# Forgetting and memory attention computed by key instead of by query, with one output product for all mixer blocks

## What is computed

```
x = x + 1/2 * swiglu_1(rms(x))
h = rms(x);  u, c_gate, b_gate, q, k, v, f_logit, q_mem = split(h @ w_in)
y_conv = b_gate * (conv_b + causal conv over 3 tokens of (c_gate * u))        # 256 columns
q, k = head_rms(q), head_rms(k)                                              # 8 heads x 64
F = cumsum(log_sigmoid(f_logit + b_f))                                       # one value per token and head
y_fox = softmax(q k^T / 8 + F_t - F_s, masked to s <= t) v                    # 512 columns
y_mem = softmax(head_rms(q_mem) mem_k^T / 8) mem_v                            # 4 heads, 256 memory tokens
x = x + concat(y_conv, y_fox, y_mem) @ w_out
x = x + 1/2 * swiglu_2(rms(x));  x = rms(x)
```

## Time and profile before

| | |
|---|---|
| time, median of 3 runs | 2314.63 us (2314.17 to 2317.61) |
| the profiled execution, its own time | 2306.02 us |
| its span | 2304.2 us |
| PE busy | 92% of the span |
| DVE, ACT, POOL busy | 51%, 33%, 17% |
| mean granted clock of PE | 0.96 of full speed |
| mixer (817 to 1499 us of the span) | 682 us |

### The profile page before, as it was taken

The page is one execution under the profiler, slowest core; times in us unless marked ns, Lnnn a source line. Parts: engine busy times, 40 slices in busy tenths (PEclk is TensorE's granted clock), DMA queues, the critical chain, the costliest instruction groups (busy, mean ns, idle before and its releaser), DMA issues.

```text
span 2304.2 us, 40450 instructions
## 1 busy us (share of the span) xinstructions
PE 2118.3 (92%) x15785; PEld 2027.2 (88%) x15785; DVE 1183.0 (51%) x2332; ACT 749.0 (33%) x1385; POOL 388.5 (17%) x290
## 2 busy tenths in 40 slices
PE   4599999999999879899999989966999999999996
PEld 4599999999999879779788777765999999999996
DVE  6855566556320063545544556677655665643103
ACT  5332222324221241152433433443232232433213
POOL 0000000004444422221221223100000000143440
PEclk7799999999999989899999998987999999999997
DMA  4512222228532114311020210132222222385222
GB/s 150 140 57 83 84 81 88 70 77 301 175 123 92 46 29 37 62 29 56 23 79 23 55 51 18 44 113 83 77 73 84 84 75 90 116 297 168 89 68 85
DMA packets 206427, 205.78 MB, mean 89 GB/s; under 512 B 15864, under 2 KB 150264, under 8 KB 206016
## 3 DMA queue, kind: packets, MB, share of 16 engines
q1 hardware_dynamic: 206272, 203.59, 29.1%
HBM read 161.87 MB, written 41.69 MB: 88 GB/s over the span
## 4 chain that ended last, share of the span: by engine, by line
PE 52%; DVE 5%; issue 2%; ACT 2%; DMA 1%; another core or an unknown queue 0%; POOL 0%; DVEq 0%; ACTq 0%; SPq 0%
PE banks L256 14%; PE banks L257 14%; PE banks L258 14%; PE banks L1994 3%; PE banks L2033 3%; PE banks L2014 2%; PE banks L1761 1%; PE banks L1945 1%; DVE xT L1563 1%; DVE row_bias L1641 1%; DMA x_again<-x_spill 1%; DVE w_raw L1708 0%; DVE hforms_lo L1415 0%; DVE hforms_f L1399 0%; PE banks L2096 0%
## 5 line engine op out<-in xcount | busy, mean ns | idle before, releaser
L256 PE MATMUL banks<-hforms_hi,w_hi 128*128 128x264 f32 x2112 | 604.2, 286 | 65.7 <-DVE hforms_lo L1415 44.6
L257 PE MATMUL banks<-hforms_lo,w_hi 128*128 128x264 f32 x2112 | 606.2, 287 | 0.0
L258 PE MATMUL banks<-hforms_hi,w_lo 128*128 128x264 f32 x2112 | 603.0, 286 | 0.0
L256 PEld LDWEIGHTS banks<-hforms_hi,w_hi 128*128 128x128 f32 x2112 | 402.3, 190 | 68.9 <-issue 35.8
L747 POOL TENSOR_TENSOR w_lo<-w_raw,w_hi 128x1024 fp32r<-128x1024 f32 x88 | 219.6, 2498 | 1311.8 <-ACT w_hi L992 1311.8
L258 PEld LDWEIGHTS banks<-hforms_hi,w_lo 128*128 128x128 f32 x2112 | 402.1, 190 | 0.0
L257 PEld LDWEIGHTS banks<-hforms_lo,w_hi 128*128 128x128 f32 x2112 | 401.1, 190 | 0.0
L256 PE MATMUL banks<-acts_a,w_hi 128*128 128x264 f32 x896 | 255.3, 285 | 1.8 <-DVE acts_a L1433 1.8
L258 PE MATMUL banks<-acts_a,w_lo 128*128 128x264 f32 x896 | 255.2, 285 | 0.0
L257 PE MATMUL banks<-acts_a,w_hi 128*128 128x264 f32 x896 | 255.1, 285 | 0.0
L992 ACT ACTIVATE w_hi<-w_raw 128x1024 fp32r<-128x1024 f32 x88 | 93.3, 1060 | 347.8 <-PE banks L258 305.4
(11 more groups left out here) (260 smaller groups left out, 4135.7 us busy)
## 6 DMA issues: line engine op xcount, KB each, us to landing
w_raw<-in_w_ffn_down SPq DMA_DIRECT2D x88, 512.0 KB, 4.0
w_raw<-in_w_ffn_gate SPq DMA_DIRECT2D x48, 512.0 KB, 5.2
w_raw<-in_w_ffn_up SPq DMA_DIRECT2D x48, 512.0 KB, 5.2
act_rows<-act_f SPq DMA_DIRECT2D x44, 528.0 KB, 2.8
acts_f<-act_rows SPq DMA_DIRECT2D x44, 528.0 KB, 5.0
w_raw<-in_w_in SPq DMA_DIRECT2D x20, 512.0 KB, 6.1
x_spill<-xT SPq DMA_DIRECT2D x4, 2112.0 KB, 9.3
xT<-x_spill SPq DMA_DIRECT2D x2, 4224.0 KB, 16.6
```

Source lines behind the costliest of these rows:

```text
L256: eng.matmul(out, w_hi, x_hi, start=first, stop=False, skip_group_check=added)
L257: eng.matmul(out, w_hi, x_lo, start=False, stop=False, skip_group_check=added)
L258: return eng.matmul(out, w_lo, x_hi, start=False, stop=last, skip_group_check=added)
```

## The change

The change rewrites the mixer from the first conv block to the start of feed-forward 2. The feed-forward code is untouched. In parts:

**Output products to the end.** No mixer block has its own output product. Each result `mix_f32` is stored as rows in memory (`mix_rows`, by `store_mix` on SP). At the end SP loads w_out (eight blocks of 128 rows) and the results back; ACT rounds both (`w_out_hi`, `mix_hi`), POOL subtracts for the low parts of w_out, DVE for those of the results (`mix_lo`). One stretch of PE then does three chunks, in each of them eight column blocks d with the blocks of rows (0 to 3), (4 to 6), (7) summed in eight banks; 576 matmuls as before, but 24 additions to x in place of 192. x goes out to memory at the start of the mixer (`x_spill`) and comes back at the end, since the room is used.

**Stacked operands.** With 64 rows a head, a head's high and low parts fit one above the other in 128 partitions. `k_hi_twice` (KS1) holds k_hi in both halves, `k_lo_and_one` (KS2) k_lo in one half and a row of ones in the other; `q_hi_lo` (Q1) q_hi and q_lo, `q_hi_and_max` (Q2) q_hi and one row with minus the row maximum. KS1 with Q1 gives k_hi*q_hi + k_hi*q_lo in one float32r matmul, KS2 with Q2 gives k_lo*q_hi and subtracts the maximum. ACT makes the rounded copies (L1118, L1126), DVE the second copy of k_hi and the low parts.

**Maxima from a one-pass product.** For each of the 18 units PE makes KS1 times Q1 alone (`scores`, L2055, L2058), one query tile by all its keys; DVE takes the maximum with -F as before, but writes nothing that is used (`scores_minusF`). PE turns the column of maxima to a row (`turn_max`), ACT copies it, negated, into Q2 (`maxima`).

**Scores by key.** The scores are then made again with keys on the partitions: 28 blocks of one key tile by up to 512 queries for a fox pair, 12 for a memory pair (`key_blocks`, `keyed`, two matmuls and the mask). ACT takes the exponential with bias -F of the key (L1163) straight into `probsT`, four buffers. No probability is turned.

**Weighted sum with the row sum in it.** `v_and_ones` (VO) holds v of a head in 64 columns and ones in the other 64. `weigh` multiplies it (stationary) by the probabilities (up to 512 columns, plain float32); one half of the bank is the result by feature, the other half the sum in every row. ACT makes a rough reciprocal by Ln and Exp (`sum_rough`), DVE one correction step and the product in three instructions (`mixed`). No result is turned.

**Moves.** The maxima products of head 1 stand among the key blocks of head 0. The fox loop is unrolled. DVE's forget scan stands among the norms of the first fox pair; the turn of log f and -F by token, which stood before the fox loop, comes after the key tiles of the first fox pair. The second conv block uses banks shifted by one. The memory's products 2 and 3 wait for the memory operand (`mp["dve"]`), where this wait stood after product 2. FFN2's means wait for the 24 additions.

The diff, cut to its core:

```diff
-        qz = sb("qT_by_head", [P, PAIR, T], F32, ms_)
...
+        KS1 = sb("k_hi_twice", [P, PAIR, KEYS], F32R, ax)
+        KS2 = sb("k_lo_and_one", [P, PAIR, KEYS], F32R, ax)
+        VO = sb("v_and_ones", [P, NT + 1, PAIR, P], F32, ax)
...
+        Q1 = sb("q_hi_lo", [P, PAIR, T], F32R, xs)
+        Q2 = sb("q_hi_and_max", [P, PAIR, T], F32R, xs)
...
+        PRT = sb("probsT", [P, 4, 512], F32, xs)
...
+        mix_rows = nc.dram_tensor("mix_rows", (KT, P, T), F32, kind="Internal").ap()
...
+        UNITS = [(PT, 0), (PT, 1)] + [(t, j) for j in range(PAIR) for t in range(PT)]
...
+        def key_blocks(kind):
+            r = []
+            for j in range(PAIR):
+                for e in range(PT if kind == "fox" else 2):
+                    for c in range(2):
+                        lo = max(P * e, 512 * c) if kind == "fox" else 512 * c
+                        if lo < 512 * c + 512:
+                            r.append((j, P * e, P, e, lo, 512 * c + 512 - lo, 4 * j + c, lo - 512 * c, e == 0,
...
+        HOOK = {"fox": [[t] for t in range(PT)] + [[]] * 4, "mem": [[0, 1], [2, 3], [4, 5], [6, 7]]}
+        TURN2 = {"fox": 9, "mem": 3}
...
+            def store_mix(b):
+                sp.dma_start(mix_rows[b], mixf[:, :]).then_inc(MIX["stored"], 16)
...
+                def q_hi(c):
...
+                    for q in (Q1, Q2):
+                        for j in range(PAIR):
+                            act.activation(q[half_rows(j), j, s:s + w], qT[half_rows(j), s:s + w], ACT.Copy)\
+                                .then_inc(A["qhi"], 1)
...
+                def exps(n):
...
+                    act.wait_ge(A["keyed"], b0 + n + 1)
+                    if b0 + n >= 4:
+                        act.wait_ge(A["pv"], b0 + n - 3)
...
+                        act.activation(dst, src, ACT.Exp, bias=Ftok[0:kr, vo, it * PAIR + j:it * PAIR + j + 1])\
+                            .then_inc(A["expd"], 1)
...
+                def sum_rough(x):
...
+                    act.activation(lr[r, 0:w], bank(b, w)[r], ACT.Ln).then_inc(A["rough_sum"], 1)
...
+                    act.activation(lr[r, 0:w], lr[r, 0:w], ACT.Exp, scale=-1.0).then_inc(A["rough_sum"], 1)
...
-                        dve.tensor_tensor_reduce(B["prob"][0:rows, a % 2, 0:W], sc, nF[0:rows, j, k0:k0 + W], 1.0,
-                                                 -3e38, ALU.add, ALU.max, m).then_inc(A["smax"], 1)
...
+                        dve.tensor_tensor_reduce(junk[0:rows, 0:w], PS[0:rows, b:b + w], nF[0:rows, j, k0:k0 + w], 1.0,
+                                                 -3e38, ALU.add, ALU.max, m).then_inc(A["smax"], 1)
...
+                def mixed(x):
...
+                    dve.tensor_tensor(lt[l, 0:w], PS[l, b:b + w], lr[l, 0:w], ALU.mult).then_inc(A["mixed"], 1)
...
+                    dve.scalar_tensor_tensor(lt[r, 0:w], lt[l, 0:w], -2.0, lr[l, 0:w], ALU.add, ALU.mult)\
+                       .then_inc(A["mixed"], 1)
...
+                    dve.scalar_tensor_tensor(mixf[r, s:s + w], PS[r, b:b + w], -1.0, lt[r, 0:w], ALU.mult, ALU.mult)\
+                       .then_inc(A["mixed"], 1)
...
-                        mm = pe.matmul(PS[0:rows, base + c:base + c + n], qz[:, j, s:s + rows],
-                                       B["kT"][:, k0 + c:k0 + c + n], start=True, stop=not diag)
...
+                        mm = pe.matmul(PS[0:rows, base + c:base + c + cw], Q1[:, j, s:s + rows],
+                                       KS1[:, j, k0 + c:k0 + c + cw], start=True, stop=not diag)
...
-                def turn_probs(a):
...
-                def turn_o(t):
...
-                        mm = pe.matmul(bank(6 + j, HD, rows), B["pT"][0:kr, a % 2, c:c + rows], v,
-                                       start=(e == 0), stop=(e == len(kb) - 1))
...
+                def keyed(n):
...
+                    if n >= 2:
+                        pe.wait_ge(A["expd"], b0 + n - 1)
...
+                    pe.matmul(dst, KS1[:, j, kc:kc + kr], Q1[:, j, q0:q0 + w], start=True, stop=False)
+                    mm = pe.matmul(dst, KS2[:, j, kc:kc + kr], Q2[:, j, q0:q0 + w], start=False, stop=not diag)
...
+                def weigh(n):
...
+                    pe.wait_ge(A["expd"], b0 + n + 1)
...
+                    pe.matmul(PS[:, 512 * ob + oc:512 * ob + oc + w], VO[0:kr, vo, j, :], PRT[0:kr, (b0 + n) % 4, 0:w],
+                              start=first, stop=last, skip_group_check=True).then_inc(A["pv"], 1)
...
+                for n in range(NB[kind] + 1):
+                    if n < NB[kind]:
+                        keyed(n)
+                    if n:
+                        weigh(n - 1)
+                    if n < len(HOOK[kind]):
+                        for t in HOOK[kind][n]:
+                            scores(2 + PT + t)
+                    if n == TURN2[kind]:
+                        turn_four(1, 0)
+                        turn_four(1, 1)
...
-                out_product(kind, it, (6, 12, 18), (0,))
-                turn_o(NT - 1)
-                out_product(kind, it, (6, 12, 18), (1, 2))
...
+            for c, (s, w) in enumerate(CHUNKS):
+                for ks in ((0, 1, 2, 3), (4, 5, 6), (7,)):
+                    for d in range(KT):
...
+                        for k in ks:
...
+                            mm = split3(pe, bank(OBANK[d], w), h[:, k % 4, ds], l[:, k % 4, ds], hh[:, k, s:s + w],
+                                        hl[:, k, s:s + w], k == 0, k == KT - 1)
```

1275 lines of the change are left out of this document (673 added, 602 removed).

## The result

The changed kernel takes 2341.98 us (median of 4 runs, 2340.95 to 2343.32), against 2314.4 us of the kernel before in the same runs: ratio 1.0121, 95% interval 1.0103 to 1.0138. It is slower by 28 us where 24 less were forecast. The span of its profiled execution is 2338.9 us, 34.7 more than before.

What follows compares the result with a forecast made beforehand. PE, busy 92% of the span, was taken as the bound. Conv -31.7, fox -71.7, memory and output product +79.2 summed to -24.2 us: 2290 us on the median 2314.6, range 2266 to 2316.

Steps and rivals of the forecast that it cites:

- The two prices: PE matmuls: rounded hi/lo operands pass once at 0.453 ns a column, plain f32 four times at 1.7 ns.
- the work of a pair: PE's work in a fox pair's attention after the change: 34.6 us against some 47 before.
- a rival at 2.6 us a pair: Narrow one-pass products in fox pairs cost the four-pass rate: 2300 us in all, chance 10%.
- below the column rate nothing can lie: Narrow one-pass products, 32 to 160 columns, some 40 a fox pair, were priced by columns as the lower end.
- The first maxima product starts 3.8 us after the projections: Fox pair: PE waits for ScalarE's copies, through some 3.5 us after PE, with 0.5 us of transposes to do.
- The clock: Rival: PE's pauses start each pair's loop at 1.2 GHz, 6 us in six pairs, 36 in all: 2326, chance 10%.
- I take 3.6 us of pauses: Fox loop over 28 key blocks: 28.9 us of PE work plus these pauses, 0 to 10 possible.
- First fox pair: 7 us above the other pairs' 83.8: about 4 for the forget scan in VectorE's queue, some 3 for -F.
- POOL's new memsets and the copy of x to memory lie under the products of these blocks: Conv stage: this added work, like storing each block's result, was taken as hidden under PE's products.
- Memory pairs: Two pairs of 62.0 and 60.6 us, each with 7.4 us of copies after the last projection; loop 14.5 in the first.
- Conv, -31.7: Conv stage to the first fox product: 98.3 us instead of 130, with two output products gone.
- Output products: All 576 products in one piece at the end: 92.0 us, 0.6 for the last addition, 2.2 waiting for FFN2's squares.

Runs made afterwards that it cites:

- e1: Changed kernel with GpSimd's split of the next block's weights made after all 18 maxima of the pair, not right after the last projection: 2340.2 us, ratio 1.0108.
- e6: Changed kernel with ScalarE's four copies of the first chunk of q after a fox pair's seventh projection, not its eighth: 2342.4 us, ratio 1.0137.
- e12: e11 with GpSimd's split of the next weights after the maxima, and 12 and 26 extra matmuls in the pauses behind the projections: 2301.9 us, ratio 0.9943.
- e2: Changed kernel with a filler, extra PE matmuls nobody uses, in the pauses before the maxima products and first key block of every pair but the first: 2335.2 us.
- e9: Changed kernel with key block scores made two blocks ahead of the weighted sum, not one, in head 1 and behind it: 2343.0 us, ratio 1.0134.
- e5: e3 with the first pair's cached keys and values loaded ahead of the two small stores of the conv state: 2337.5 us, ratio 1.0104.
- e3: Changed kernel with ScalarE and VectorE waiting for GpSimd's constants at the parts of k, not at the first fox pair's start: 2345.3 us, ratio 1.0127.
- e4: Changed kernel with two buffers in turn for the rough reciprocal of a sum, not one: 2333.9 us, ratio 1.0081.
- e15: e14 with 4 extra matmuls in a memory pair's pause in place of 12: 2292.1 us, ratio 0.9907.
- e13: Kernel before, with the first split of w_out moved behind the squares and sums of the mixer's first norm: 2303.8 us, ratio 0.9954.
- e14: e12 with the first two q chunks' parts made between a memory pair's projections, and 12 extra matmuls in its pause: 2291.0 us, ratio 0.9909.
- e11: e10 with the extra matmuls of e2, 15 in a fox and 34 in a memory pair's pause, then 4 and 3: 2304.9 us, ratio 0.9965.
- e10: Changed kernel with the edits of e4, e5 (which contains e3), e6 and e9 together, without extra matmuls: 2321.9 us, ratio 1.0036.

## Why the prediction was wrong

By its own steps, in the profiled execution: forecast -24.2, measured +34.7, so 58.9 us are missing.

- **The two prices, and the work of a pair: right but for narrow products.** A block of 512 columns in memory's head 1 takes 1.32 us from start to start, by columns 1.33. The narrow ones were a rival at 2.6 us a pair ("if they took the f32 rate"); they cost 0.11 to 0.12 us each, at 32 columns as at 128. With 8 products and 4 sums of 32 columns and 8 products of 128 columns (0.12 against 0.058) that is some 2 us a pair. So "below the column rate nothing can lie" stood, and taking the column rate was the wrong end. The Trainium skill (TensorE: Matmul & The Clock Gate, Back-to-back issue gap) has about 81 ns at 128 columns; 110 to 120 were measured.
- **"The first maxima product starts 3.8 us after the projections": 5.7.** ScalarE's last copy of q ends 4.1 us after them, where I had ScalarE done with all its copies after 3.5; VectorE's last two low parts, which end 1.3 us after that, were not costed. GpSimd's split, which I had looked at only for its own length, was in their way (e1: -1.4; 5.3 in the first memory pair), and the order of ScalarE's copies was worth as much (e6: -1.4; both, in e12: -2.5).
- **The clock: the rival was right in its mechanism and I gave it 10%.** I set, two stretches half busy that kept 1.00, against the earlier trace rows, pauses that did not. The new pause has no work in it at all for 5 us, so the earlier trace rows was its neighbour. The price was 6 us a pair in the text, 2 in the maxima stage and 4 in the loop; alone the filler gave back 3.2, 2.0 and 1.2, and in the combined kernel 4 to 7.5 a fox pair. The rule of the Trainium skill that I set beside it (TensorE: Matmul & The Clock Gate, HAM oscillation) was borne out (0.51 granted behind the pause). It is not the whole of the miss, but it decided what the other repairs were worth: e1 and e6 gained nothing without it.
- **"I take 3.6 us of pauses" in the loop, 0 to 10 possible: 7.1, of 36.0.** 1.2 are clock (e2), some 0.9 the one block of lead (e9), 2 the narrow products; the other 3 are not taken apart.
- **First fox pair: +17.2 us, 8.4 of them those of every pair.** Of the rest, I had 4 us for the scan in VectorE's queue and 3 for -F. The 3 were right (PE waits 2.7 us for the row of maxima behind the load of -F). The 4 were not seen: up to the pair's last projection PE has no wait but the two below; with both gone, in e5, it waits 2.3 us for VectorE's norm of q. Not seen: ScalarE's first wait for GpSimd's constants, of which the last stands behind the storing of the conv state, and that the turn of the cached keys moved up to the second projection while its load stayed behind that same storing on SyncE (e3, e5). That "POOL's new memsets and the copy of x to memory lie under the products of these blocks" was true of their work and not of the wait in front of the last.
- **Memory pairs: +12.9 and +5.2 us.** One buffer of sums is 5.2 and 4.2 of it (e4; 1.1 of the 4.2 in the second pair's projections): the sum had the loop at 14.5 without asking what the second Ln waits for. GpSimd's lock is 5.3 of the first pair's pause (e1), of which 2.8 were won in the pair. The 7.4 us of copies were about right (8.4 measured in the second pair) and could have been moved (e15). The second pair's projections took 3.4 us more than the 19.5 of the sum. PE came to them from six us at a clock of 0.78, with a wait of 2.2 us at their end, and then had half the clock for 6 us, 18 products 0.32 us apart in place of 0.174, which alone is 2.6 us:

```profile
1363.00:1369.00 6.00, 3.81 (x17) 2.74 (x18) 2.97 (x5) 2.88 (x8) 0.00 (x0) 0.78 0.00 0
1369.00:1375.00 6.00, 6.00 (x21) 6.00 (x21) 2.28 (x8) 0.84 (x4) 0.00 (x0) 0.50 0.39 115
```

- **Conv, -31.7: right**, in its terms too (98.2 us against 98.3; PE waits 6.6 us for the second block's weights where I had 7). **Ahead of it: forecast 0, came -5.7**, since the first split of w_out no longer stands ahead of the norm's sums on GpSimd (e13). I counted output products and not what was queued in front of them. **Output products: +2.4**, of which 2.3 us lie in the first third of the first chunk (19.0 us for 96 products of 0.174), where low parts come one by one; the wait for the squares was 2.5, forecast 2.2.

The missing 58.9 us sum up as 42.3 in fox, 18.1 in memory, 4.2 behind them and -5.7 ahead. Open: what makes the clock fall at a pair's end at one time and not at another, where the rest of the gain of e14 over e12 comes from, and the 3 us of a fox loop named above.

## What to carry to other kernels

Where a change puts a stretch behind a stage in which TensorE has nothing at all to do, price that stretch at the lower clock, and look for work (even idle work) to lay into it before shortening anything else: in fox, pauses shortened by 1.4 us gave nothing that can be told until the clock was held. Count a moved step with all that it waits for and all that stands in its queues: here most terms that missed had their operations right, and a buffer, a lock or a store at the head of a queue wrong.

## What the runs showed of the hardware

- A 64 KB load issued on one queue behind two stores of 1 KB in 4-byte pieces (12.1 and 19.2 us to landing) and three transfers of 0.5 MB: 22.8 us to landing (e3). Ahead of all five: 1.8 us (e5).
- VectorE's subtraction of two SBUF operands, 64x384: 0.55 us alone, up to 2.58 beside GpSimd's subtractions. Its reductions from PSUM kept their 1225 ns for 1024 columns, also the one at 979.3 us that lay wholly beside GpSimd's work.
- One-pass (float32r) products of 32 columns: 0.11 us from start to start with full weights of 128x128, a float32 one of 32 columns 0.24.
- 27 extra matmuls in each later fox pair and 37 in a memory pair made the kernel faster by 7 us (e2); 22 and 41 of them, together with the other repairs, by 17 us (e11 against e10).
